# An RWKV recurrence in 64x64 tiles: block-diagonal stationaries for the inverse, and an order of work written out by hand

## The reference

```python
def wkv_scan(r, w, k, v, a, b, s0, reverse):
    def step(S, xs):
        r_t, w_t, k_t, v_t, a_t, b_t = xs
        sa = jnp.einsum('bhvk,bhk->bhv', S, a_t)
        S = S * w_t[:, :, None, :] + sa[..., None] * b_t[:, :, None, :] + v_t[..., None] * k_t[:, :, None, :]
        return S, jnp.einsum('bhvk,bhk->bhv', S, r_t)
    s_T, o = lax.scan(step, s0.astype(jnp.float32), xs, reverse=reverse)
```

## Time and profile before

| | us |
|---|---|
| median of 3 runs | 3524.1 |
| lowest, highest | 3513.17, 3540.83 |
| the profiled execution | 3541.05 |
| its span | 3539.3 |

### The profile page before, as it was taken

How to read it: one execution, slowest core, us unless ns; L and a number is a source line. 1 busy time by engine, 2 the same in 40 slices (tenths; PEclk the granted TensorE clock), 3 DMA queues, 4 the chain that set the end, 5 groups by cost and what they waited for, 6 DMA issues and landing times. The chain is left out here.

```text
span 3539.3 us, 78591 instructions
## 1 busy us (share of the span) xinstructions
PE 2984.3 (84%) x35105; PEld 1728.2 (49%) x35105; DVE 1374.2 (39%) x2442; ACT 509.7 (14%) x1254; POOL 396.6 (11%) x488
## 2 busy tenths in 40 slices
PE   5899999996766878778877469995999999999993
PEld 1566676664555666666666234452333332333331
DVE  1676766673343344444443311224213222223123
ACT  2100000002231222222222211111001000000001
POOL 0100000000353222222221100000000000000000
PEclk8899999998686687887787689997999999999997
DMA  9575555552430000000000757785999999999997
GB/s 412 179 219 179 182 201 195 194 189 103 120 95 19 21 4 25 25 25 24 23 3 16 281 194 292 289 334 216 383 400 413 396 397 401 395 412 411 397 419 301
DMA packets 224700, 777.26 MB, mean 220 GB/s; under 512 B 55362, under 2 KB 119577, under 8 KB 155826
## 3 DMA queue, kind: packets, MB, share of 16 engines
q1 hardware_dynamic: 212818, 712.28, 52.2%
q0 software_dynamic: 11248, 60.87, 5.7%
q10 hardware_dynamic: 368, 0.10, 0.0%
HBM read 711.00 MB, written 62.18 MB: 218 GB/s over the span
## 5 line engine op out<-in xcount | busy, mean ns | idle before, releaser
L2135 PE MATMUL ex_ps<-experts_ring,ex_xe 128*32 128x512 f32 (+1 forms) x4608 | 678.0, 601 | 48.6 <-DMA experts_ring<-in_w_up 26.8
L2137 PE MATMUL ex_ps<-experts_ring,ex_xe 128*32 128x512 f32 (+1 forms) x1536 | 677.5, 601 | 0.0
L2135 PEld LDWEIGHTS ex_ps<-experts_ring,ex_xe 128*32 128x32 f32 (+1 forms) x4608 | 213.8, 107 | 498.1 <-issue 480.7
L476 DVE SCALAR_TENSOR_TENSOR pj_macc<-pj_mring,head_cond_t,pj_macc 128x1024 f32<-128x1024 f32 x240 | 296.9, 1278 | 183.5 <-DMA pj_mring<-in_w_ada 183.5
L2150 PE MATMUL ex_ps<-experts_ring,ex_hidt 128*32 128x512 f32 (+1 forms) x2304 | 334.6, 595 | 6.9 <-DVE ex_hidt L2217 6.9
L2152 PE MATMUL ex_ps<-experts_ring,ex_hidt 128*32 128x512 f32 (+1 forms) x768 | 334.1, 595 | 0.0
L549 PE MATMUL pj_ps<-head_hT,head_ring_in 128*128 128x320 f32 x1104 | 313.4, 437 | 5.9 <-DVE head_hT L449 3.5
L1933 PE MATMUL om_ps<-experts_ring,om_ot 128*128 128x512 f32 x640 | 287.6, 611 | 15.1 <-DMA om_ot<-scratch_o 15.1
L549 PEld LDWEIGHTS pj_ps<-head_hT,head_ring_in 128*128 128x128 f32 x1104 | 211.3, 192 | 96.6 <-DVE head_hT L449 6.3
L2239 DVE SCALAR_TENSOR_TENSOR ex_hid<-ex_hid,ex_gcol,ex_ps 80x512 f32<-80x512 f32 x16 | 11.9, 744 | 594.1 <-ACT ex_hid L2182 594.1
L2150 PEld LDWEIGHTS ex_ps<-experts_ring,ex_hidt 128*32 128x32 f32 (+1 forms) x2304 | 106.7, 106 | 226.0 <-issue 218.2
(11 more groups left out here) (359 smaller groups left out, 3999.7 us busy)
## 6 DMA issues: line engine op xcount, KB each, us to landing
experts_ring<-in_w_gate SPq DMA_DIRECT2D x128, 1024.0 KB, 19.4
experts_ring<-in_w_up SPq DMA_DIRECT2D x128, 1024.0 KB, 22.2
experts_ring<-in_w_down SPq DMA_DIRECT2D x128, 1024.0 KB, 20.9
experts_ring<-in_w_out SPq DMA_DIRECT2D x68, 1024.0 KB, 7.1
pj_mring<-in_w_ada SPq DMA_DIRECT2D x64, 1024.0 KB, 9.2
head_ring_in<-in_w_in SPq DMA_DIRECT2D x23, 2048.0 KB
ada_ring<-in_w_ada SPq DMA_DIRECT2D x16, 2048.0 KB, 20.7
scratch_z<-pj_stage POOLq DMA_DIRECT2D x19, 640.0 KB, 8.3
```

The lines of the kernel that those rows point to most:

```text
L476: a = nc.vector.scalar_tensor_tensor(acc, w, scalar, acc, ALU.mult, ALU.add)
L2135: pe.matmul(ps[rows, bank, :], xe[:, k, rows], cols, start=(k == 0), stop=(k == KD - 1))
L2137: mm = pe.matmul(ps[96:96 + rows.stop - rows.start, bank, :], xe[:, k, rows], up[:, g1], start=(k == 0), stop=(k == KD - 1))
```

## The change

All products of the recurrence now have the same tile size.

- The inverse: a chunk's matrix becomes one stationary of 64x64 for each head, whose 32x32 blocks off the diagonal are zero, with 32 moving columns: two products a chunk instead of four. For this, `near` and `far` hold the scores' blocks on and off the diagonal, copied with a factor of 0 or 1 by ScalarE (`halve`, six copies a unit), and VectorE empties every x job, the last level's too, into an `xm` of twice the width, with a mask of `kept`, which GpSimd makes once.
- The projections w/a: two stationaries of 64 columns instead of one of 128.
- The list of a unit is written out: projections first, then the five score jobs with two slots for stages behind each, `scan` behind score job 1 instead of score job 4, one slot behind each x and d job, `removal` after level 0, the exponentials in levels 2 and 3, and the scalings in levels 3 and 4. Stages are laid into slots one by one instead of by costs.
- The first stage of a unit's chain waits for less; the wait for the inverse moves to its second stage.

```diff
-        items = [("sc", 0, u), fr[0], ("sc", 1, u), fr[1], ("sc", 2, u), fr[2], ("sc", 3, u), fr[3], ("sc", 4, u)]
-        items += ["scan"] if more else []
-        fill = [("bk", 0, u), ("bk", 1, u), ("bk", 2, u), fr[4], vt[0], vt[1]]
+        fill = {0: [("bk", 0, u), ("bk", 1, u)], 1: [("bk", 2, u), s0], 2: [vt0, vt1]}
+        then = {(0, 1): ["removal"], (2, 0): ["exp_in"], (2, 1): ["exp_inv"], (3, 0): ["exp_ex", "decay", "pad_b"], (3, 1): ["pad_k"], (4, 0): ["pad_a"]}
+        items = [w0, a0, w1, a1]
+        for b in range(NCK // 2):
+            items += [("sc", b, u)] + (["scan"] if b == 1 else []) + ["slot", "slot"]
         for lv in range(LAST_LV + 1):
...
+            for k, kind in enumerate(("x", "d")):
+                for b in range(2):
+                    items += (["turn%d" % b] if (lv, kind) == (0, "x") else []) + [(kind, b, lv, u), "slot"]
+                    items += [fill[lv][k]] if lv in fill and b == 0 else []
+                items += then.get((lv, k), [])
...
+            for i in range(5):
+                for h in range(2):
+                    ch.link(nc.gpsimd.tensor_scalar(kept[:, i, h, :], join[:, i, :], half[:, h:h + 1], None, ALU.mult))
+            ch.link(nc.gpsimd.memset(kept[:, 5:7], 0.0))
...
-                        mm = pe.matmul(bank[:, 0:HALF], wa2[rows, p % 2, d, :], xwa[rows, b * HALF:(b + 1) * HALF], start=True, stop=True)
+                        for cols in HEADS:
+                            mm = pe.matmul(bank[cols, 0:HALF], wa2[rows, p % 2, d, cols], xwa[rows, b * HALF:(b + 1) * HALF], start=True, stop=True)
...
-                        for g, rows in enumerate(GROUPS):
-                            at = GROUPS[g ^ 1] if last else rows
-                            if kind == "x":
-                                h = (g + 1) % 2 if last else g % 2
-                                lhs, rhs = sc[rows, u % NS, c, 0, HB * h:HB * h + HB], tm[rows, c, :]
-                            else:
-                                lhs, rhs = xm[rows, c, :], tt[rows, c, :]
-                            mm = pe.matmul(out[at], lhs, rhs, start=True, stop=True)
+                        lhs, rhs = (lt[:, c, :], tm[:, c, :]) if kind == "x" else (xm[:, c, :], tt[:, c, :])
+                        mm = heads(bank[:, i * HB:(i + 1) * HB], lhs, rhs, True, True)
...
+            def halve(u, dst, c0, c1, other):
+
+                act.wait_ge(dve_ev, RANK[G["sc", (c1 - 1) // 2, u]])
+                for h in range(2):
+                    lt = sc[:, u % NS, c0:c1, 0, HB * h:HB * h + HB]
+                    a = nc.scalar.activation(dst[:, c0:c1, HB * h:HB * h + HB], lt, ACT.Copy, scale=half[:, (h + other) % 2:(h + other) % 2 + 1])
+                a.then_inc(halved, 1)
...
-                    nc.vector.tensor_tensor(chunks(xm, b), src, join[:, lv + 1:lv + 2, :].to_broadcast([P, BC, HB]), ALU.mult).then_inc(dve_ev, 1)
+                    n = lv + 1 if lv < LAST_LV else 5 + d
+                    nc.vector.tensor_tensor(chunks(xm, b).rearrange("p c (h k) -> p c h k", k=HB), src.unsqueeze(2).to_broadcast([P, BC, 2, HB]),
+                                            kept[:, n:n + 1].to_broadcast([P, BC, 2, HB]), ALU.mult).then_inc(dve_ev, 1)
```

More of the change, by code:

```diff
@@ L1086, in plan @@
     def plan(u):
-        fr = front_jobs(u + 1) + [None] * 5
-        vt = [("vt", b, u) for b in range(2)] if u % 2 == 0 else [None] * 2
-        more = u + 1 < NU
-        items = [("sc", 0, u), fr[0], ("sc", 1, u), fr[1], ("sc", 2, u), fr[2], ("sc", 3, u), fr[3], ("sc", 4, u)]
-        items += ["scan"] if more else []
-        fill = [("bk", 0, u), ("bk", 1, u), ("bk", 2, u), fr[4], vt[0], vt[1]]
-        for lv in range(LAST_LV + 1):
[L1095 to L1111, removed]
+        w0, w1, a0, a1, s0 = front_jobs(u + 1) or [None] * 5
+        vt0, vt1 = [("vt", b, u) if u % 2 == 0 else None for b in range(2)]
+        fill = {0: [("bk", 0, u), ("bk", 1, u)], 1: [("bk", 2, u), s0], 2: [vt0, vt1]}
[3 more added lines that the diff above has]
+            items += [("sc", b, u)] + (["scan"] if b == 1 else []) + ["slot", "slot"]
+        for lv in range(LAST_LV + 1):
+            for k, kind in enumerate(("x", "d")):
[3 more added lines that the diff above has]
+                items += then.get((lv, k), [])
+        skip = () if u + 1 < NU else ("scan", "removal", "exp_in", "exp_inv", "exp_ex", "decay", "pad_b", "pad_k", "pad_a")
+        return [i for i in items if i is not None and i not in skip]
     def chain(v, i0, i1):
@@ L1120, in sequence @@
         return [s for pair in itertools.zip_longest(old, new) for s in pair if s is not None]
-    COST = {"sc": 9, "w": 6, "a": 6, "s0": 2, "bk": 9, "vt": 6, "x": 7, "d": 7}
     def timeline(u):
         items, seq = plan(u) if u < NU else [], sequence(u)
-        total = sum(COST[i[0]] for i in items if not isinstance(i, str))
-        out, spent, placed = [], 0, 0
+        slots, out, seen, placed = items.count("slot"), [], 0, 0
         for i in items:
-            out.append(i)
-            spent += 0 if isinstance(i, str) else COST[i[0]]
-            while placed < len(seq) and (placed + 1) * total <= spent * len(seq):
+            if i != "slot":
+                out.append(i)
+                continue
+            seen += 1
+            while placed * slots < seen * len(seq):
                 out.append(seq[placed])
@@ L1154, in block_rwkv @@
         mask = sb("mask", [P, 2, 2 * CK])
-        join, first, half = sb("join", [P, 6, HB]), sb("first", [P, 2, HB]), sb("half", [P, 2])
+        join, half = sb("join", [P, 6, HB]), sb("half", [P, 2])
+        kept = sb("kept", [P, 7, 2, HB])
         reset = sb("reset", [P, T])
@@ L1191, in block_rwkv @@
         NLOAD, NLOADW = 4 * 16, 6 * 16
-        MADE = 68
+        MADE = 79
         def c3(t):
```

43 lines of the change are left out of this document (26 added, 17 removed).

## The result

The changed kernel takes 3280.28 us (median of 4 runs, 3274.61 to 3282.61) where the kernel before takes 3527.39 on the same chip (3513.17 to 3540.83): a ratio of 0.930, 95% interval 0.926 to 0.934. The direction was right, the size was missed by nearly half.

The account below looks back on a forecast made before the run. TensorE was taken as the bound, partly at half clock, plus waits. Work of 31.8 us at clock 0.85 (36.8) plus 7 of waits gave 43.8 a unit, 8.5 less over 16 units, minus 4: 3395 us, range 3310 to 3485.

Parts of the forecast that it names:

- What bounds the kernel: In the recurrence, a unit is TensorE's work, partly at half clock, plus some 11 us of waits.
- VectorE did not become the bound: Rival: VectorE's in-order queue makes levels of 5 us in the inverse, 51 us a unit, 3500 us; chance 0.10.
- The inverse job: On TensorE, 20 rows in 64x64 tiles take 0.58 us a job, against 0.60 before.
- Issue waits: In the inverse, TensorE's waits for instructions shrink with half the matmuls; 1.0 us a unit of 4.6 is left.
- The seam and the new waits: Between units the 2.4 us wait goes; new waits of 1.6 (scan), 1.0 (half 0), 0.9 (half 1) come.
- The wait behind the scan: In the score stretch, TensorE waits 1.6 us a unit for z stages queued behind the scan on VectorE.
- The 1.0 for VectorE in level 3: Two scalings raise VectorE's work in level 3 to 4.5 us against TensorE's 3.6: a wait of 1.0.
- the 1.0 for ScalarE's queue: ScalarE's six new copies, about 2.1 us a unit, are hidden but for queues: 1.0 us of waits.
- The start: In the setup, 11 more GpSimd operations, for which VectorE waits, cost 4 us once.
- The projections: Four w/a jobs a unit stay near 0.74 us each, 3.0 together, up to 4.6 if column tiles don't overlap.
- The clock: In the recurrence, the granted clock rises from 0.77 to 0.85, 30% at half speed, as waits get shorter.
- the clock nearly full: Rival: once waits are short nothing makes the clock fall; 37.3 to 40 us a unit, 3290 to 3330; chance 0.15.

Follow-up runs that it names:

- e1: Kernel before with the new order of the list and its waits, keeping the old 32x32 inverse and 128-column projections: 3390.92 us, ratio 0.961.
- e2: Changed kernel with the old order of the list (old `plan` and `timeline`), keeping the new tiles: 3393.44 us, ratio 0.962.
- e7: Changed kernel with the three scalings of the next unit behind the last level again: 3322.77 us, ratio 0.941.
- e5: Changed kernel with ScalarE's `near` copies made earlier and `far` only in level 1: 3247.46 us, ratio 0.920.
- e11: `e5` with the scan cut into two of 320 columns, behind score jobs 1 and 3: 3243.64 us, ratio 0.915.

## Why the prediction was off

**What bounds the kernel: right.** TensorE, with waits on top, before and after. VectorE did not become the bound: the stretch has it busy 366 of 560 us, and its queue shows mainly in the waits for `rw_tmp`.

**The inverse job: right.** 0.58 us forecast, priced by the weight load, 0.56 measured. The tiles save next to nothing in TensorE time, as said; their gain is the supply of instructions and what hangs on it.

**Issue waits: too careful.** 1.0 us a unit was left of 4.6 (the 76 us named beside it are 4.8), since a level would just meet the pace of supply; what came is under 0.1. `e1` and `e2` show that the tiles decide this and the order doesn't, and that half the matmuls in an inverse job were few enough.

**The seam and the new waits: right in place and near in size, one of them in part by luck.** The seam keeps 0.15 to 0.55 us where 0 was forecast. The wait behind the scan was worked out as 1.6 and is 1.40. That sum took the scan at its old length, and it fell to 1.49, since at its new place GpSimd's start of the inverse no longer runs beside it:

```profile
1407.12 1.49 DVE L1595 TENSOR_TENSOR_SCAN rw_cs<-rw_reset,rw_sg 128x640 f32<-128x640 f32 x1
```

With 1.49 in place of 2.03 the same working gives about 1.0, so some 0.4 us of the wait are not in it. Ahead of half 0 it was 1.0, and it is 1.04; ahead of half 1 0.9, and it is 1.41, since ScalarE's copies end last there. The 1.0 for VectorE in level 3 came out as 0.16 (2.6 us in 16 units), and of the 1.0 for ScalarE's queue 0.4 came (6.4 us for `rw_sg`, `rw_usb` and the like). All waits: 7 forecast, 4.7 in the rows, about 5 with what the modelled ends hide.

**The start: right.** 4 us were allowed, and TensorE's wait for `rw_sg` at the start grew by 4.9; before, then changed:

```profile
1058.32 0.48 PE L1369 MATMUL rw_rot<-rw_eye,rw_sin 64*64 64x64 f32 x4 [11.07 <-ACT rw_sg L1483]
```

```profile
1058.35 0.48 PE L1366 MATMUL rw_rot<-rw_eye,rw_sin 64*64 64x64 f32 x4 [15.93 <-ACT rw_sg L1478]
```

From the first projection (1044.73 before, 1039.99 changed) to the first score product it is 27.0 and 30.9 us; `e1`, without the eleven operations, has 26.2. The first score product stands at nearly the same time, 1071.68 and 1070.91, only because the part ahead of the recurrence ended 4.7 us sooner, in `e1` too.

**The projections: mis-sized.** 3.0 us for the four, 1.5 measured. The term failed because 0.74 was read from a job that stands alone, and was used for four that stand together. The text asked whether the two column tiles of one job run side by side, and not whether a w and an a job do, on their two halves of the rows; they do, with 128 stationary columns as well, so it is the order that won the 1.5 us and not the tiles. The change of tile size is the smaller part of the 0.74: the lone projection starts 0.21 us behind a stage product (1493.97 - 1493.76), where one of the same size starts after 0.12. The Trainium skill ("TensorEngine Tiling (Array Packing)", Key Properties) says that switching the tiling mode drains the engine; the trace agrees with these 0.09 us.

**The clock: the step that failed.** 0.85 was chosen, 0.96 measured. The text gave the clock nearly full a chance of 0.15, with the time 3290 to 3330, and argued with the inverse stretch of 0.81; but that stretch had its own issue waits in it, which the change removed, so it was no bound for what came after. What `e1` and `e2` show is that either half of the change alone brings the 0.85, and the other half then brings as much again. And `e7` shows what the choice had left out: 28 to 31 us of waits more bring the clock from 0.96 to 0.92, with TensorE's own work untouched, so waits that fall from 11 to 5 us a unit move it by more than 0.08.

With the measured terms the sum closes: work 31.8 - 1.5 = 30.3 (the jobs of 0.56 take off another 0.4), 29.9 / (1 - 0.09 x 0.45) = 31.2, and 5 of waits: 36.2, as measured. Of the 7.6 us a unit between 43.8 and 36.2, the work is 2.2 (1.9 divided by the clock's 0.865), the waits 2.0, and the clock the remaining 3.4. Times 16 that is 122 us; the medians miss by 115. The case of a clock nearly full, 3290 to 3330, missed too: it had the clock right and the projections at 3.0.

## What to carry to other kernels

Price an operation from a row with the neighbours that it will have, not only of its own kind: alone and in a row it differed here by a factor of two, since two jobs on different halves of the rows ran side by side. Where TensorE shows half clock between waits, count a wait that goes as worth more than its length (`e7`: 42 us of time for 31 us of wait; near full clock, in `e5`, that no longer showed), and don't take the clock of a stretch for a ceiling when the change removes that stretch's own waits. In an engine whose queue is in order, moving a long operation ahead trades one victim for another; cut it, and put something between the pieces (`e11`, likely 4 to 9 us).

## What the runs showed of the hardware

- Waits for "issue" go with the number of matmuls and loads in a stretch of some us and not with the order of work: 65.1 us over the inverses of `e1`, 0.5 in `e2`, at the same clock; the instruction queue moved 224 packets before and 175 after. The mean over a long stretch does not tell it: `e11` has 13600 matmuls in 510 us and no such wait, the kernel before 12686 and 48 us of them, since its inverse jobs have 40 records where the others have 20.
- Half the moving columns make a product of 64 stationary columns no shorter: 20 rows with 32 moving columns take 0.56 us, 4 rows with 64 take 0.117, 0.028 and 0.029 a row.
- A projection of 320 moving columns alone takes 0.74 us. Four in a row, two on each half of the rows, take 1.43 us with 128 stationary columns and 1.51 with 64, and 1.52 with the two of one half ahead of the others.
- A scan of 640 columns on VectorE took 2.03 us in 15 of the 16 scans of the kernel before and in every one of `e2`, and GpSimd worked beside each of these for 1.95 us (the start of the inverse). It took 1.49 in the first scan of the kernel before and in every one of the changed kernel, `e1` and `e5`, with nothing on GpSimd beside it; two of 320 took 0.82 and 0.81. GpSimd pays too: its step L1317 takes 1.59 us beside the scan and 0.52 elsewhere, and the same step is 0.52 throughout in the changed kernel.
